# State-space input matrices turned by VectorE instead of TensorE in a hybrid S5 and attention layer

## What is computed

```python
a_bar = jnp.exp(lam * dt)
b_bar = ((a_bar - 1.0) / lam)[:, :, None] * lax.complex(B_re, B_im)
bu = jnp.einsum('blgc,gpc->blgp', uf, b_bar)
bu = bu.at[:, 0].add(a_bar[None] * h0)
_, h = lax.associative_scan(combine, (a_seq, bu), axis=1)
y = jnp.real(jnp.einsum('blgp,gcp->blgc', h, c)) + D * uf
```

## Time and profile before

| | |
|---|---|
| median of 3 runs | 2914.99 us (2913.64 to 2916.24) |
| the profiled execution | 2914.06 us |
| its span | 2912.3 us |
| granted TensorE clock, mean | 0.997 |
| instructions in the span | 47939 |
| packets of 16 DMA engines | 448498, 354.32 MB |

### The profile page before, as it was taken

The page is one execution under the profiler, slowest core; times in us unless marked ns, Lnnn a source line. Parts: engine busy times, 40 slices in busy tenths (PEclk is TensorE's granted clock), DMA queues, the critical chain, the costliest instruction groups (busy, mean ns, idle before and its releaser), DMA issues.

```text
span 2912.3 us, 47939 instructions
## 1 busy us (share of the span) xinstructions
PE 2869.9 (99%) x18500; PEld 2822.6 (97%) x18500; DVE 1407.8 (48%) x2627; ACT 987.1 (34%) x1206; POOL 457.3 (16%) x1127
## 2 busy tenths in 40 slices
PE   6999999999999999999999999999999999999998
PEld 5999999999999999999999999999999999999987
DVE  7725454463545455354445534545566543422256
ACT  6235225313521631452253144126421411211142
POOL 7500330230032033004203300510000200000000
PEclk9999999999999999999999999999999999999999
DMA  6233333333433333333333333333549854332273
GB/s 189 69 111 111 107 86 106 108 78 103 125 90 100 98 109 83 106 113 96 101 103 101 81 104 110 98 102 102 176 150 293 267 186 149 104 120 72 79 253 125
DMA packets 448498, 354.32 MB, mean 122 GB/s; under 512 B 83330, under 2 KB 401170, under 8 KB 446482
## 3 DMA queue, kind: packets, MB, share of 16 engines
q1 hardware_dynamic: 448274, 351.36, 40.6%
HBM read 250.34 MB, written 88.34 MB: 116 GB/s over the span
## 4 chain that ended last, share of the span: by engine, by line
PE 90%; POOL 2%; DMA 2%; DVE 2%; SPq 2%; issue 1%; ACT 1%; POOLq 0%; DVEq 0%; ACTq 0%
PE acc L1898 78%; PE acc L2157 5%; PE side L2028 2%; PE side L2045 2%; DMA t_sig_ga<-work 1%; PE side L1865 1%; PE side L1998 1%; PE side L1999 0%; POOL prologue L1220 0%; POOL prologue L1221 0%; DMA work<-work 0%; SPq L526 0%; DMA w_raw<-in_w_branch_a 0%; PE side L2016 0%; PE side L2131 0%
## 5 line engine op out<-in xcount | busy, mean ns | idle before, releaser
L1898 PE MATMUL acc<-x_high,w_high 128*128 128x344 f32 (+1 forms) x5312 | 1708.7, 322 | 3.1 <-DVE w_low L1443 1.6
L1898 PE MATMUL acc<-x_high,w_low 128*128 128x344 f32 (+1 forms) x5312 | 1689.5, 318 | 0.0
L1898 PE MATMUL acc<-x_low,w_high 128*128 128x344 f32 (+1 forms) x5312 | 1688.9, 318 | 0.0
L1898 PEld LDWEIGHTS acc<-x_high,w_high 128*128 128x128 f32 x5312 | 998.0, 188 | 5.2 <-issue 3.3
L1898 PEld LDWEIGHTS acc<-x_low,w_high 128*128 128x128 f32 x5312 | 997.9, 188 | 0.7
L1898 PEld LDWEIGHTS acc<-x_high,w_low 128*128 128x128 f32 x5312 | 997.3, 188 | 0.0
L1443 DVE TENSOR_TENSOR w_low<-w_raw,w_high 128x1024 fp32r<-128x1024 f32 x233 | 287.9, 1236 | 558.9 <-ACT w_high L968 556.1
L968 ACT CAST w_high<-w_raw 128x1024 fp32r<-128x1024 f32 x232 | 243.0, 1048 | 928.8 <-PE acc L1898 823.4
L1313 POOL COPY work<-s_tables 128x28 f32 x16 | 3.3, 208 | 1417.0 <-DVE work L1608 1169.7
L1622 DVE TENSOR_SCALAR work<-side,sb_bias_all 128x128 f32<-128x128 f32 (+3 forms) x64 | 52.3, 818 | 164.9 <-PE side L2045 164.8
L1033 ACT ACTIVATE work<-work 128x128 f32<-128x128 f32 (+3 forms) x64 | 43.7, 683 | 241.0 <-DVE work L1632 241.0
(11 more groups left out here) (330 smaller groups left out, 2655.3 us busy)
## 6 DMA issues: line engine op xcount, KB each, us to landing
w_raw<-in_w_in SPq DMA_DIRECT2D x160, 512.0 KB, 4.1
w_raw<-in_w_out SPq DMA_DIRECT2D x48, 512.0 KB, 3.9
work<-t_sig_ga SPq DMA_DIRECT2D x24, 516.0 KB, 4.4
out<-work SPq DMA_DIRECT2D x22, 512.0 KB, 3.8
t_sig_gb<-stage SPq DMA_DIRECT2D x16, 516.0 KB, 5.2
t_sig_ga<-stage SPq DMA_DIRECT2D x16, 516.0 KB, 4.7
t_sig_ga<-work SPq DMA_DIRECT2D x16, 516.0 KB, 4.4
work<-t_sig_gb SPq DMA_DIRECT2D x16, 516.0 KB, 3.6
```

The costliest lines, as they stand in the source:

```text
L1898: ins = mm(acc[s][:, a, 0:n], w[b][:, kk, :], x[:, kx, c0:c0 + n], start=start, stop=stop)
```

## The change

The four transposes on TensorE at BT, ScalarE's copy to B1T and the semaphores between them go. VectorE transposes the 32 x 32 blocks of M1 (128 x 512) into `m_turned_tile`, in half 0 between the third and the fourth doubling of the tables at TURN, in half 1 at step 23. It waits there for `m_ready` and, in half 0, for the store of the last iteration's attention output. SyncE stores the tile to a new DRAM tensor with four DMAs (`b_out`: 32 partitions each, runs of 512 bytes), waits for their landing, and loads it into B1T with four (`b_back`: 128 partitions, runs of 128 bytes). In half 0 both stand between `ahead(2)` and `u_groups`; in half 1 the store stands at the end of chunk number 6's transfers and the load ahead of the Toeplitz copies. ScalarE at BT now waits for `m_ready` itself. TensorE at KM takes over the waits that stood at BT, and at PQ it waits for the load's landing. ScalarE's and VectorE's writes of Kt wait for the transpose, since Kt lies over M1.

```diff
--- before.py
+++ after.py
@@ -147,6 +147,7 @@
     side_flat = side[:, :, :].rearrange("p a b -> p (a b)")
 
     t_turned, t_w = dram("t_turned", [2, P, SEQ]), dram("t_w_turned", [P, SEQ])
+    t_b = dram("t_b_turned", [4, P, HG * 32])
     t_sza, t_y = dram("t_silu_za", [FT, P, TOK]), dram("t_y", [FT, P, TOK])
     t_sga, t_sgb = dram("t_sig_ga", [KT, P, TOK]), dram("t_sig_gb", [KT, P, TOK])
     t_oz, t_m = dram("t_oz", [HEADS, P, SEQ]), dram("t_merged", [KT, P, TOK])
@@ -200,7 +201,8 @@
     N2 = c.take(HG * 9 * GC).rearrange("p (g q) -> p g q", g=HG)
     Er = c.take(512).rearrange("p (g j) -> p g j", g=HG)
     Ei = c.take(512).rearrange("p (g j) -> p g j", g=HG)
-    B1T = c.take(512).rearrange("p (g s) -> p g s", g=HG)
+    B1T_flat = c.take(512)
+    B1T = B1T_flat.rearrange("p (g s) -> p g s", g=HG)
     turn_at = c.at
     swapped_p = c.take(512)
     Toep = c.take(512).rearrange("p (g q) -> p g q", g=HG)
@@ -218,6 +220,7 @@
     ysT = c.take(P, NEW)
     fo = c.take(P, HG)
     B0T = c.take(P)
+    m_turned_tile = c.take(512)
     c.at = WORK - (12 * HG + 6 * HG + NEW)
     pw = c.take(12 * HG)
     turn = c.take(6 * HG).rearrange("p (a g) -> p a g", a=6)
@@ -299,8 +302,8 @@
     s5_in, seed_in, seed_ready, s_seed_ready, seed_out, m_ready, n_ready, n_in, ha_ready = [sem(s) for s in
         ("s5_in", "seed_in", "seed_ready", "state_seed_ready", "seed_out", "s5_m_ready", "s5_n_ready", "s5_n_in", "s5_ha_ready")]
     b0_ready, b0_mm, b0t_ready = sem("s5_b0_ready"), sem("s5_b0_mm"), sem("s5_b0t_ready")
-    b_mm, bt_ready, k_mm, kt_ready, kt_pad, toep_in = [sem(s) for s in
-        ("s5_b_mm", "s5_bt_ready", "s5_k_mm", "s5_kt_ready", "s5_kt_pad", "s5_toep_in")]
+    b_turned, b_sent, b_in, k_mm, kt_ready, kt_pad, toep_in = [sem(s) for s in
+        ("s5_b_turned", "s5_b_sent", "s5_b_in", "s5_k_mm", "s5_kt_ready", "s5_kt_pad", "s5_toep_in")]
     u_sent, ug_in, yj_sent, yj_in, pq_mm, v_ready, y_mm, yj_ready, fin_ready, p_copied, t_ready, swap_in = [sem(s) for s in
         ("s5_u_sent", "s5_ug_in", "s5_yj_sent", "s5_yj_in", "s5_pq_mm", "s5_v_ready", "s5_y_mm",
          "s5_yj_ready", "s5_fin_ready", "s5_p_copied", "s5_scanned", "s5_swapped_in")]
@@ -546,6 +549,17 @@
                 sp.wait_ge(y_gelu, i + 1)
                 sp.dma_start(t_y[bass.ds(i, 1)].rearrange("a p n -> (a p) n"), xy).then_inc(y_sent, 16)
 
+            def b_out(hf):
+                sp.wait_ge(b_turned, i * 2 + hf + 1)
+                for q in range(4):
+                    sp.dma_start(t_b[q].rearrange("(j a) n -> a j n", a=32),
+                                 m_turned_tile[q * 32:(q + 1) * 32].rearrange("a (j n) -> a j n", j=4)).then_inc(b_sent, 16)
+
+            def b_back(hf):
+                sp.wait_ge(b_sent, i * 128 + 64 * (hf + 1))
+                for q in range(4):
+                    sp.dma_start(B1T[:, :, q * 32:(q + 1) * 32], t_b[q].rearrange("p (g n) -> p g n", g=HG)).then_inc(b_in, 16)
+
             def attn_load():
 
                 sp.wait_ge(y_sent, (i + 1) * 16)
@@ -592,6 +606,8 @@
                 if cn == CHUNKS - 1 and not last:
                     s5_params(0)
                 if cn == 2:
+                    b_out(0)
+                    b_back(0)
                     u_groups()
                 if cn == 3:
                     toeplitz(0)
@@ -606,7 +622,9 @@
                     s5_seeds(1)
                     y_rows(0)
                     s5_states(0)
+                    b_out(1)
                 if cn == 7:
+                    b_back(1)
                     toeplitz(1)
                     sp.wait_ge(k_turned, i + 1)
                     sp.dma_start(t_turned[0], stage[0][:, 0:SEQ]).then_inc(stage_sent[0], 16)
@@ -858,7 +876,7 @@
 
 
 
-    TURN, BT, KM, PQ, SCAN, ROT, YM, YS = (4, 20), (8, 24), (11, 27), (13, 30), (15, 32), (17, 34), (18, 36), (19, 37)
+    TURN, B_TURN, BT, KM, PQ, SCAN, ROT, YM, YS = (4, 20), (4, 23), (8, 24), (11, 27), (13, 30), (15, 32), (17, 34), (18, 36), (19, 37)
     YN, YT = 38, 40
     QK_LO = (18, 26)
     K_TURN, V_TURN, VT, KTR, ZB_AT = 26, 35, 45, 57, 44
@@ -988,12 +1006,14 @@
                     evacuate(i, ZB)
                 for hf in range(2):
                     if p == BT[hf]:
-                        act.wait_ge(b_mm, 2 * i + hf + 1)
-                        nc.scalar.copy(B1T, side[:, 0, :].rearrange("p (g s) -> p g s", g=HG)).then_inc(bt_ready, 1)
+                        act.wait_ge(m_ready, 2 * i + hf + 1)
+                        if hf == 0:
+                            act.wait_ge(oz_ready, 8 * i + PRIMED)
                         nc.scalar.copy(B0.rearrange("p (g c) -> p g c", g=HG), M1[:, :, 0:2 * GC]).then_inc(b0_ready, 1)
                     if p == KM[hf]:
                         act.wait_ge(k_mm, 2 * i + hf + 1)
                         act.wait_ge(b0_ready, 2 * i + hf + 1)
+                        act.wait_ge(b_turned, 2 * i + hf + 1)
                         nc.scalar.copy(Kt[:, :, 7 * GC:15 * GC], side[0:GC, 0, :].rearrange("p (g q) -> p g q", g=HG)).then_inc(kt_ready, 1)
                         act.wait_ge(b0_mm, 2 * i + hf + 1)
                         nc.scalar.copy(B0T, side[:, 1, 0:P]).then_inc(b0t_ready, 1)
@@ -1522,6 +1542,12 @@
                        V.tensor_tensor(both, er, ei, ALU.mult))
                     ch(V.tensor_tensor(er, sq[:, 0, :], sq[:, 1, :], ALU.subtract), V.tensor_tensor(ei, both, both, ALU.add))
 
+        def b_turn(i, hf):
+            dve.wait_ge(m_ready, 2 * i + hf + 1)
+            if hf == 0:
+                dve.wait_ge(oz_sent, i * 16 + PRIMED)
+            V.transpose(m_turned_tile, m_flat[:, 0:512].rearrange("p (g j a) -> p j g a", g=HG, a=32)).then_inc(b_turned, 1)
+
         def phase_a(i, last):
             ch = Chain(dve, dve_chain, i * DVE_A + base)
 
@@ -1539,12 +1565,20 @@
                         dve.wait_ge(s5_in, i * 128 + 64)
                         if hf == 1:
                             dve.wait_ge(y_mm, 2 * i + 1)
-                        turning(i, hf, ch, range(5))
+                        if hf == 0:
+                            turning(i, hf, ch, range(3))
+                            b_turn(i, hf)
+                            turning(i, hf, ch, range(3, 5))
+                        else:
+                            turning(i, hf, ch, range(5))
                     if p == TURN[hf] + 4:
                         turning(i, hf, ch, range(5, 7))
+                    if p == B_TURN[hf] and hf == 1:
+                        b_turn(i, hf)
                     if p == KM[hf]:
                         dve.wait_ge(k_mm, 2 * i + hf + 1)
                         dve.wait_ge(b0_ready, 2 * i + hf + 1)
+                        dve.wait_ge(b_turned, 2 * i + hf + 1)
                         V.memset(Kt[:, :, 0:7 * GC], 0.0).then_inc(kt_pad, 1)
                     if p == PQ[hf]:
                         dve.wait_ge(pq_mm, 2 * i + hf + 1)
@@ -1963,19 +1997,13 @@
                 if p % 4 == 3:
                     last_op.then_inc(chunk_used, 1)
                 for hf in range(2):
-                    if p == BT[hf]:
-                        pe.wait_ge(m_ready, 2 * i + hf + 1)
+                    if p == KM[hf]:
+
+                        pe.wait_ge(n_ready, 2 * i + hf + 1)
                         if hf == 0:
                             pe.wait_ge(oz_ready, 8 * i + PRIMED)
                         else:
                             pe.wait_ge(ys_ready, 2 * i + 1)
-                        for g in range(HG):
-                            last_op = tr(side[:, 0, g * P:(g + 1) * P], M1[:, g, :], ident[:, :])
-                        last_op.then_inc(b_mm, 1)
-                    if p == KM[hf]:
-
-                        pe.wait_ge(n_ready, 2 * i + hf + 1)
-                        pe.wait_ge(bt_ready, 2 * i + hf + 1)
                         for g in range(HG):
                             last_op = one(side[:, 0, g * P:(g + 1) * P], M1[:, g, :], N1[:, g, 0:CH * GC])
                         last_op.then_inc(k_mm, 1)
@@ -1984,6 +2012,7 @@
                     if p == PQ[hf]:
 
                         pe.wait_ge(kt_ready, 2 * i + hf + 1)
+                        pe.wait_ge(b_in, (2 * i + hf + 1) * 64)
                         if hf == 0:
                             pe.wait_ge(ug_in, i * 192 + 192)
                         for g in range(HG):
```

## The result

The changed kernel takes **2926.76 us** (median of 6 executions, 2921.82 to 2929.16) against 2915.11 us for the kernel before on the same chip (6 executions, 2912.78 to 2919.32). The ratio is 1.0039, with a 95% interval of 1.0029 to 1.0050: slower by 0.4%. The forecast was 2920.5, with a range of 2911 to 2931. So the side and the range held, and the size came out 6 us short; the narrower band of the forecast, 2916 to 2925, was missed by 1.8 us, and the chances had leaned a little to no change (0.46 against 0.44 for slower).

What follows compares the result with a forecast made beforehand. TensorE, busy 99% of the span, was taken as the bound, with SyncE's chain tight in half 0. Terms -3.5 (half 1's transposes) + 6.7 (iterations 1 to 7) + 3.2 (iteration 0) = +6.4 us: 2920.5, range 2911 to 2931.

Steps and rivals of the forecast that it cites:

- The 0.44 us for a group's transposes: TensorE: dropping a group's four transposes saves 0.44 us, 7.0 us over 16 groups, gained only in half 1.
- the matrices late in iteration 0: Iteration 0: GpSimd's matrices come only at 76.50, VectorE waits, u's store goes 4.15 us late; +3.2 us.
- From 2.6 us to about 15 us in 8 waits: TensorE's waits at half 0's output product for VectorE's rotated states should rise this much.
- X: Delay of SyncE's store of u (t_u) in half 0, iterations 1 to 7: 1.1 us, bounds 0.2 and 3.5.
- a delay X moves L1573 by X less 0.15: Half 0: VectorE's rotated states (L1573) come later by this, TensorE standing still; +6.7 us over iterations 1 to 7.
- Issue: SyncE, half 0: with the added stores, landing and loads, t_u is issued at 333.2 instead of 332.46, 0.75 us later.
- backlog: t_u's packets stand behind 2048 short ones of the four loads: 0 to 2 us, taken as 0.35.
- The landing of 1.7 us: SyncE waits for the last store of the turned matrices, which lands after 1.7 us, as y rows do.
- Half 1 keeps this: 3.5 us gained, because of its 4.1 us to spare: Half 1's rotated states are ready 4.1 us before TensorE's output product, so 8 x 0.44 us is gained.
- A: Rival: the loads' 128-byte runs back up the queue shared with t_u; X = 2.5, +17.6 us, about 2931.5; chance 0.17.
- B: Rival: output-product wait is scatter or SyncE makes up its loss; -6.6 us, about 2907.5; chance 0.09.
- C: Rival: the round trip hides, landing and issue at their fastest, X near 0.2; -1 us, about 2913; chance 0.06.

Runs made afterwards that it cites:

- second and fourth kernels: Kernel before plus VectorE's transposes and SyncE's stores, wait and loads, TensorE's transposes kept: 2927.94 us; changed kernel, half 0's four loads issued behind u's stores: 2912.70 us.
- the one with step 28: Changed kernel with half 0's loads within u's round trip, parameters behind the first swap, half 1's kernel matrices formed at step 28 instead of 27: 2904.56 us.

## Why the prediction was right on the side and short on the size

**The mechanism held.** The 0.44 us for a group's transposes, VectorE's part at nothing, the matrices late in iteration 0, all waits in half 0 and none in half 1: these are in the trace. "From 2.6 us to about 15 us in 8 waits" came out as 14.6 in 8 for the matmuls. By the sum's own steps TensorE was to lose 7 x 0.44 (it arrives earlier) + 6.7 + 3.2 = 13.0 us ahead of half 0's output products; it lost 14.6. The second and fourth kernels show by what: SyncE's order.

**X was too small, and the chain took up more of it than was read.** X is the delay of the t_u issue. It was put at 1.1 us for iterations 1 to 7 and at 4.15 for iteration 0; measured are 2.0 in the mean (1.36 to 3.16) and 6.7. And "a delay X moves L1573 by X less 0.15" did not hold: in iterations 1 to 7 the rotated states are later by X less 0.8 in the mean (8.5 us together, from 14.2 of delay), in iteration 0 by X less 2.9, not 0.9. The two errors nearly cancel: 8.5 us for the predicted 6.7, and 3.7 for 3.2. That this term of the sum came out near its size is luck. Where the chain gives way: u's round trip, from t_u's issue to the group loads, is 0.4 us shorter in the mean (in iteration 1, 343.37 - 340.19 = 3.18 for 336.09 - 332.46 = 3.63; in iteration 0 it is 1.5 shorter). The rest is time that SyncE had stood waiting in the kernel before: up to 0.8 us for the source of the Toeplitz copies in iterations 1 to 7 and 1.0 in iteration 0, and 0.8 and 1.3 us ahead of the weight chunk in iterations 6 and 7. The prediction had read the wait for the source in iteration 1, 0.2 us. Before the change the copies start 10.17 to 10.92 us after t_u in iterations 1 to 7, and 9.26 to 9.57 after the change.

**Why X was too small.** Issue was put at 0.75 us and backlog at 0.35. The loads take 0.65 to 0.69 each, and 0.83 in iteration 1, not the 0.5 of the output seeds, which have the same 512 runs. The number of runs was a poor guide: a parameter load of the kernel before, 256 runs of 64 bytes, already takes longer than those.

```profile
350.29 0.60 SPq L433 DMA_DIRECT2D work<-in_ssm_B_im  x1
```

The stores take the 0.45 each that were predicted in six iterations, but 0.68 and 0.66 in two (5 and 6). DMA issues of the kernel after (count, KB each, median us from issue to landing):

```profile
t_b_turned<-work SPq DMA_DIRECT2D x64, 64.0 KB, 1.8
work<-t_b_turned SPq DMA_DIRECT2D x64, 64.0 KB, 2.5
```

The landing of 1.7 us was right in the median (1.8); the two late ones, in iterations 0 and 4, put 1.7 us more each straight into t_u's delay, and they stand before the two longest waits. Of a backlog behind t_u's issue the trace shows nothing, since u's round trip did not get longer. t_u's own issue takes 0.62 us behind the loads, where it took 0.34.

**Two more steps failed.** "Half 1 keeps this: 3.5 us gained, because of its 4.1 us to spare" looked only at the output product. Nine steps earlier TensorE takes up GpSimd's matrices with 0.13 us to spare, and 1.9 of the 3.5 us were lost there. The kernel without transposes and the one with step 28 show it. And the sum had no term for what a wait does to the matmuls behind it: 4.9 us in the profiled execution. Predicted +6.4, with these two +13.2, with the 1.6 us more that TensorE lost ahead of the output products +14.8, as in the working above; the execution measured +14.0.

**The rivals.** A (the queue backs up, 2931) is nearer in time, and its delay, 2 us or more, is nearly the measured mean of 2.0. Its cause isn't seen: the delay is there before t_u is issued, in the time that the loads take SyncE to issue and in late landings. Whether those longer issues are themselves the queue holding SyncE back, no run tells. B's time was wrong, but its point was half right: it wanted 1 us to spare between t_u and swap one, and 0.8 is the mean that the chain took up. The rows held against it were those of one iteration. The delay was larger than what was to spare, and so the kernel is slower and not faster. C wanted a delay near 0.2; the smallest one measured is 1.36.

**What stays open:** what decides whether the clock falls behind a wait. It is not the same from one execution to the next. Of the five executions of the kernel with SyncE's part and the transposes, two took 2922.4 and 2922.5 us at a mean granted clock of 0.997 and 0.998, the other three 2927.9 to 2931.6 at 0.995. It may well be why the kernel after spreads over 7 us; that was not tested.

## What to carry to other kernels

Work taken from the busiest engine is gained only as far as its next wait has slack, and there is one such wait per producer: list them all, GpSimd's too, not only the one that looks tight. What a chain of issues has to spare is read from every iteration and not from one: here it was 0.2 us in the one that was read, and the chain took up 0.8 in the mean. A round trip through DRAM that is added to an in-order queue belongs inside a wait which that queue has anyway; the same eight transfers cost 14 us in one place and nothing in the other. And a stall of TensorE of two to five microseconds may cost 1.6 to 2.9 us more than its length.

## What the runs showed of the hardware

- TensorE went on at a granted clock of 1.2 GHz for 3.4 to 6.2 us behind eleven single waits of 1.81 to 4.6 us, in two kernels, though it was busy for nearly all of the execution (mean clock 0.995 and 0.991). It did not behind the five waits of 1.74 us and less in the first of them, nor behind one of 3.05 us in another kernel.
- The time SyncE takes to issue a transfer is not fixed by its shape. The store of u took 0.34 us in the kernel before and 0.62 in all eight iterations of the kernel after, behind loads of 512 short runs. The small store behind it mostly took 0.43, but 1.30 and 1.55 in two of eight iterations of the kernel with the loads moved, and 1.41 in one iteration of the kernel without transposes, where no such loads stand near it; what made those long is not shown.
- VectorE's 128x512 transpose takes 0.71 us in all 16 places beside GpSimd's work, the same as the eight of the earlier trace rows, beside which GpSimd did nothing.
